# Sums of weight blocks of seven-product pairs formed on GpSimd instead of VectorE

## What is computed

```python
u = rmsnorm(h, norm_w)
proj = einsum('btd,dc->btc', u, w_in)          # w_in: 4096 x 24576
(a_q, a_f, a_i, a_g, c_b, c_c, c_h, c_g, g_a, g_b) = split(proj)
... # y_a: HGRN2 recurrence in chunks; y_b: short causal convolution; both 256 x 2048
z_a, z_b = y_a @ w_branch_a, y_b @ w_branch_b  # 2048 x 4096 each
merged = sigmoid(g_a + bias_a) * z_a + sigmoid(g_b + bias_b) * z_b
h = h + merged @ w_out                         # 4096 x 4096
return rmsnorm(h, final_norm_w)
```

## Time and profile before

| | |
|---|---|
| median of 3 runs | 2887.46 us (2885.36 to 2888.29) |
| the profiled execution's own time | 2886.71 us |
| its span, first to last instruction | 2885.0 us |
| mean granted TensorE clock | 0.998 of full speed |
| TensorE busy | 99% |
| VectorE, ScalarE, GpSimd busy | 65%, 45%, 0% |
| DMA | 196 GB/s mean |

### The profile page before, as it was taken

The page is one execution under the profiler, slowest core; times in us unless marked ns, Lnnn a source line. Parts: engine busy times, 40 slices in busy tenths (PEclk is TensorE's granted clock), DMA queues, the critical chain, the costliest instruction groups (busy, mean ns, idle before and its releaser), DMA issues.

```text
span 2885.0 us, 39229 instructions
## 1 busy us (share of the span) xinstructions
PE 2858.6 (99%) x12989; PEld 2367.6 (82%) x12989; DVE 1888.1 (65%) x2085; ACT 1289.4 (45%) x1372; POOL 6.7 (0%) x22
## 2 busy tenths in 40 slices
PE   8999999999999999999999999999999999999998
PEld 7888888888888788888887888888888888888886
DVE  6566766676667645555469686776868777755454
ACT  5443444344444444333445454454545445444443
POOL 0000000000000000000000000000000000000000
PEclk9999999999999999999999999999999999999999
DMA  7555555555555566565556666666666666666665
GB/s 236 185 178 168 173 176 175 168 173 178 175 171 175 186 193 192 191 191 189 189 182 205 197 222 200 212 210 204 213 199 220 198 214 207 240 203 213 215 204 201
DMA packets 428998, 564.13 MB, mean 196 GB/s; under 512 B 25617, under 2 KB 287874, under 8 KB 428930
## 3 DMA queue, kind: packets, MB, share of 16 engines
q1 hardware_dynamic: 428930, 563.25, 60.9%
HBM read 555.28 MB, written 7.86 MB: 195 GB/s over the span
## 4 chain that ended last, share of the span: by engine, by line
PE 97%; DVE 2%; DMA 0%; issue 0%; DVEq 0%; ACT 0%; ACTq 0%; SPq 0%
PE PS L1120 24%; PE PS L1122 24%; PE PS L1121 24%; PE QL L1245 6%; PE QL L1247 6%; PE QL L1246 6%; PE PS L1245 2%; PE PS L1247 2%; PE PS L1246 2%; PE QL L1151 2%; DVE QS L620 0%; PE QL L1128 0%; DVEq L599 0%; DMA RP<-in_w_in 0%; ACT QS L387 0%
## 5 line engine op out<-in xcount | busy, mean ns | idle before, releaser
L620 DVE TENSOR_TENSOR QS<-RP,QS 128x1024 fp32r<-128x1024 f32 x800 | 976.3, 1225 | 852.3 <-ACT QS L387 836.3
L387 ACT ACTIVATE QS<-RP 128x1024 fp32r<-128x1024 f32 x800 | 845.1, 1059 | 1222.5 <-PE PS L1122 1135.3
L1120 PE MATMUL PS<-QS,U 128*128 128x512 f32 x2560 | 1009.7, 394 | 7.8 <-DVE QS L620 5.2
L1122 PE MATMUL PS<-QS,U 128*128 128x512 f32 x2560 | 998.8, 390 | 0.0
L1121 PE MATMUL PS<-QS,U 128*128 128x512 f32 x2560 | 998.0, 390 | 0.0
L1120 PEld LDWEIGHTS PS<-QS,U 128*128 128x128 f32 x2560 | 481.7, 188 | 108.4 <-issue 5.2
L1122 PEld LDWEIGHTS PS<-QS,U 128*128 128x128 f32 x2560 | 481.5, 188 | 101.3
L1121 PEld LDWEIGHTS PS<-QS,U 128*128 128x128 f32 x2560 | 482.0, 188 | 96.5
L1245 PE MATMUL QL<-QS,U 128*128 128x512 f32 x688 | 267.9, 389 | 0.0
L1247 PE MATMUL QL<-QS,U 128*128 128x512 f32 x688 | 267.7, 389 | 0.0
L1246 PE MATMUL QL<-QS,U 128*128 128x512 f32 x688 | 267.6, 389 | 0.0
(11 more groups left out here) (217 smaller groups left out, 1861.9 us busy)
## 6 DMA issues: line engine op xcount, KB each, us to landing
RP<-in_w_in SPq DMA_DIRECT2D x1024, 256.0 KB
RP<-in_w_in SPq DMA_DIRECT2D x256, 512.0 KB
RP<-in_w_out SPq DMA_DIRECT2D x128, 512.0 KB
RP<-in_w_branch_a SPq DMA_DIRECT2D x64, 512.0 KB
RP<-in_w_branch_b SPq DMA_DIRECT2D x64, 512.0 KB
XS<-in_x SPq DMA_DIRECT2D x8, 512.0 KB, 5.6
XR<-in_x SPq DMA_DIRECT2D x8, 512.0 KB, 4.5
out_dram<-H SPq DMA_DIRECT2D x8, 512.0 KB, 3.9
```

Source lines behind the costliest of these rows:

```text
L387: act.activation(WS[s][:, :, 0:OW], RAW[s][:, :, :], ACT.Copy).then_inc(hi_ready, 1)
L620: dve.tensor_tensor(WS[s][:, :, OW:2 * OW], RAW[s][:, :, :], WS[s][:, :, 0:OW], ALU.subtract).then_inc(lo_ready, 1)
L1120: pe.matmul(bank, top, w[:, k, 0:OW], start=at_k == 0, stop=False)
L1122: op = pe.matmul(bank, low, w[:, k, 0:OW], start=False, stop=at_k == n_tiles - 1)
```

## The change

The instructions that form the four sums leave VectorE's `seven` and are issued by GpSimd, in a program of its own that goes through the eight passes and their seven S units. GpSimd takes over the waits for the raw chunks and for the ring's slot, and the two counts of t_sum. The first sum instruction, which on VectorE was one of 1024 columns, becomes two of 512. VectorE, in place of the sums, waits for the second t_sum of its unit before the low halves of line 952. GpSimd starts once v_ready is counted, before the first pass. Nothing else differs: order and size of the loads, ScalarE, TensorE, the ring.

```diff
@@ block.gpsimd, after the constants
+            def seven_sums_of_weights(i, u, n_th):
+
+                chunk, n = MERGE_CHUNK + MERGE * i + 2 * u, FIRST[u]
+                s = 2 * u % RING
+                w12, w11, w22, w21 = [RP[s // 2][:, q, :] for q in range(4)]
+                sums = [QF[:, (n + 3 + q) % QRING, OW:2 * OW] for q in range(4)]
+                for t in (s, s + 1):
+                    pool.wait_ge(raw_loaded[t], (chunk - s) * (16 * KC // RING) + 16 * KC)
+                if n + 6 >= QRING:
+                    pool.wait_ge(block_used, (N_BLOCKS - 1) * i + (n + 6 - QRING + 1))
+                pool.tensor_tensor(sums[0], w11, w12, ALU.add)
+                pool.tensor_tensor(sums[1], w22, w12, ALU.add).then_inc(t_sum, 1)
+                pool.drain()
+                pool.tensor_tensor(sums[2], sums[0], w22, ALU.add)
+                pool.drain()
+                pool.tensor_tensor(sums[3], sums[2], w21, ALU.add).then_inc(t_sum, 1)
+
+            def merge(i):
+                n_th = 0
+                for u, (kind, _) in enumerate(UNITS):
+                    if kind == "S":
+                        seven_sums_of_weights(i, u, n_th)
+                        n_th += 1
+
+            pool.wait_ge(v_ready, 1)
+            merge(0)
+            with pool.Fori(1, NM) as i:
+                merge(i)
@@ block.vector, seven
-                w12, w11, w22, w21 = [RP[s // 2][:, q, :] for q in range(4)]
-                sums = [QF[:, (n + 3 + q) % QRING, OW:2 * OW] for q in range(4)]
-                for t in (s, s + 1):
-                    dve.wait_ge(raw_loaded[t], (chunk - s) * (16 * KC // RING) + 16 * KC)
-                if n + 6 >= QRING:
-                    dve.wait_ge(block_used, (N_BLOCKS - 1) * i + (n + 6 - QRING + 1))
-                for q, count, done in runs(n + 3, 2):
-                    op = dve.tensor_tensor(QF[:, q:q + count, OW:2 * OW], RP[s // 2][:, 1 + done:1 + done + count, :],
-                                           w12.unsqueeze(1).broadcast_to([P, count, OW]), ALU.add)
-                op.then_inc(t_sum, 1)
-                after()
-                dve.tensor_tensor(sums[2], sums[0], w22, ALU.add)
-                after()
-                dve.tensor_tensor(sums[3], sums[2], w21, ALU.add).then_inc(t_sum, 1)
                 dve.wait_ge(hi_ready, chunk + 2)
+                dve.wait_ge(t_sum, 2 * N_SEVEN * i + 2 * n_th + 2)
```

## The result

The changed kernel takes 3079.11 us (median; 3078.25 to 3081.57), before stood at 2886.89: a ratio of 1.0666 (95% interval 1.0653 to 1.068), 192 us slower. The direction is the one that was forecast, the size is not: 3079 lies 69 us above the forecast of 3010 and above the end of the range, 3075.

The account below looks back on a forecast made before the run. TensorE was taken as the bound, with 0.29 us of slack in the raw buffer's loop. Seven passes of 1.7 + 6 x 2.2 + 0.75, plus 12.9, gave 122 us more: 3010 us, range 2965 to 3075.

Parts of the forecast that it names:

- the price of the add: GpSimd's two-input add of 128x512: estimated 1.23 us from memset and affine_select, taken as 1.2, far end 1.7.
- Clock held: Forecast case: adds 1.05 to 1.4 us, four sums 4.3 to 6.2, granted clock not falling; 2966 to 3070 us, chance 0.60.
- The rival: TensorE's clock falls after most waits, seven products take 1.7 us more: another 66 us, 3076; chance 0.12.
- my idle stretch of 2.2 us: TensorE's steady idle time, from start to start, before each seven-product pair, six times in each of eight passes.
- the chain: GpSimd's four adds and two drains in series: 5.1 us plus 0.1 handover, against 2.70 on VectorE.
- the first pass: Waits for VectorE's copies, then for sums, in the first of eight passes: 12.9 us added in all.
- the loop below it: Ring's loop with slow seven products after a fallen clock: 13.5 us, then the longer of the two loops.
- The ring's loop at full clock: Sums wait for the preceding seven-product pair on TensorE to free a ring slot: 11.8 us around, shorter than the raw buffer's.
- the raw buffer's: Loop of landing, sums, low halves and release: 9.91 us before, 12.41 after, against TensorE's 10.20; +2.2 us a pair.
- First pair of a pass: First seven-product pair, its data already landed: low halves end 2.5 us later, TensorE waits 1.7 us more.
- End of a pass: VectorE combines gates and prepares first branch weights after the last sums; TensorE's lead is lost: +0.75 us.
- The overlap with the convolution: In the first pass, the convolution beside line 827 may run against GpSimd's reads: 0 to 3 us more, taken as 0.

Follow-up runs that it names:

- early low halves: The changed kernel, but VectorE writes the raw blocks' low halves before waiting for GpSimd's sums, and those of the sums after: 3007.36 us, ratio 1.0413.

## Why the prediction was wrong in size

**What held.** TensorE bound the kernel and a relieved VectorE gave nothing back; the loss lies in the merge alone; VectorE idles for GpSimd; where the landing came last, the sums start 5.3 to 5.9 us after the low halves' end, 5.49 on average (12 cases), where 5.42 was taken; and the price of the add, worked out from memset and affine_select as 1.23 us and taken as 1.2, measured 1.29, or 1.25 from start to start. The 1.12 us beside it was a quarter of the 4497 ns that the Trainium skill (GPSIMD Engine Reference, Performance versus the Vector engine) gives for 2048 columns. The measured 2.15 ns a column and 0.19 us would make 4.59 us of 2048 columns, an estimate that agrees with the page within about 2%; quartering it left three quarters of the fixed part out.

**The step that failed: the clock.** "Clock held" stood in the forecast case with a chance of 0.60, and the sum had no term for the clock; that most of the stretches fall was a rival with 0.12, priced at 3076. The rival is what happened, 31 of 48 times. I had put my idle stretch of 2.2 us between one of 1.80 us with the clock up and one of 2.45 after which it fell, and left it there; an interval between two readings is no evidence for its harmless end. With the clock held by zero matmuls the kernel takes 3034, well inside the range. So of the 69 us missed, 45 are the clock; the 24 left are the chain and the first pass, below. That the rival's 3076 lies so near 3079 is in part luck: it took every spacing as long and gave the clock 66 us where 45 were measured, and it lacks the 24 of the chain and the first pass.

**The size of that rival, corrected.** A slow stretch lengthens the way from the low halves' end to the next sums from 5.20 to 6.79 us, by 1.6 where 1.7 was priced. What was too short is the loop below it: 5.53 + 1.76 + 6.79 = 14.08, where I had 13.5.

**Two terms too small.** (1) *The chain*: 5.1 + 0.1 predicted, 5.53 measured, made of 1.25 + 1.45 + 1.44 + 1.39: the drains cost 0.2 from start to start, the add was 0.05 to 0.1 more, the last one counts in full. 0.33 x 56 = 18 us. (2) *The ring's loop at full clock*: 11.8 predicted, 12.48 measured; 0.33 of the gap is the chain, and from the low halves' end to the next sums it is 5.20 us, not 4.76 + 0.1, in part because the spacing of starts leaves out the end of the last matmul (0.39 us where 0.23 was counted). That put the ring's loop close behind the raw buffer's, and is why shortening the landing changed so little.

**The small terms.** First pair of a pass: TensorE waits 1.98 us, predicted 1.7. End of a pass: in the run with nine zero matmuls TensorE waits for the low halves of line 649 14 times and 9.9 us in all, before it was 7 times and 5.4 us; 0.64 for each of the seven more, predicted 0.75. In the changed kernel itself it doesn't show (7 times, 5.7 us): the last seven products of a pass are slow in seven of the eight passes (clock 0.76), and a TensorE that is late at the branches waits less. First pass: 84.7 us from first to last sums instead of 64.4, +20 where 12.2 was forecast for this stretch (12.9 less the end's 0.75). The wait for the copy, now line 855, grew from 1.80 to 4.7 us, predicted 2.5 more, measured 2.9. Three of the six spacings hold a slow stretch (the first is in the row below, the others begin at 1548 and 1575 us with the same mean of 0.76), about 1.5 us each. The overlap with the convolution, taken as 0, happened once: GpSimd's second add beside VectorE's line 983 took 2.27 us, and line 983 twice 3.46 in all instead of 2.35. The same overlap is in the run with nine zero matmuls, where line 983 is 985, and there its spacing is 13.64 us beside 12.61 of its neighbours: 1.0 us. The rest fits the longer chain. The rows, three of the changed kernel and one of the run with nine zero matmuls:

```profile
1521.00:1528.00 7.00, 7.00 (x24) 5.61 (x25) 4.52 (x8) 1.49 (x1) 0.30 (x1) 0.76 0.58 186
1539.22 3.46 DVE L983 TENSOR_TENSOR QS<-RP,QS 128x1024 fp32r<-128x1024 f32 x2
1541.56 2.27 POOL L385 TENSOR_TENSOR QF<-RP 128x512 f32<-128x512 f32 x1
...
1544.98 2.27 POOL L386 TENSOR_TENSOR QF<-RP 128x512 f32<-128x512 f32 x1
```

**What stays open.** What decides between a stretch that loses the clock and one that does not. Waits of the same 1.98 us stand on both sides: that at 1698.77 left the clock up, and the one before it, in the rows of TensorE and of the stretch below, did not; its spacing was 14.10 us. What the runs show is that waits of 1.3 us on average nearly always keep the clock (one long spacing, behind 1.90), that waits of 1.54 on average and 1.7 at most (early low halves) always did, and that those of about 2.0 and more lose it in two of three cases.

```profile
1684.67 0.69 PE L1260 MATMUL PS<-QS,U 128*128 128x512 f32 x1 [1.98 <-DVE QS L967]
1684.00:1691.00 7.00, 6.33 (x21) 5.03 (x22) 5.16 (x5) 2.70 (x3) 0.00 (x0) 0.76 0.69 217
```

## What to carry to other kernels

An engine at 0% is not free help: look for the loop that the moved work stands in (landing, work, release, landing) and its slack, here 0.29 us of 10.2, and multiply the slower engine's time by the passes of that loop. List every loop that the step lies in: here the second was 0.2 to 0.3 us behind the first, so that shortening the first alone was worth 10 us at most. When a sum leaves TensorE idle for about 2 us again and again, as here, price the fallen clock into the forecast itself, and test it with a few zero matmuls ahead of the wait.

## What was not expected of the hardware

Extra matmuls of zeros made the kernel faster, 45 us for 224 of them as well as for 504. GpSimd and VectorE, each reading two operands of SBUF, exclude each other so strictly that overlapping them brought nothing in these runs: 1.75 became 2.63 us while 1.29 became 2.60. GpSimd's two-input add costs 2.15 ns a column and 0.19 us, which is 1.29 us for 512 columns where VectorE takes 0.69.
